# Weights of one product added in SBUF in the last two groups of a two-block kernel, some loads and steps reordered

## The reference

```python
def second_block(x, p, ...):
    h = rmsnorm_2(x, attn_norm_g); proj = h @ w_in
    ...
    merged = sigmoid(g_a) * (y_a @ w_up_a) + sigmoid(g_b) * (y_b @ w_up_b)
    x = x + merged @ w_o
    h = rmsnorm_2(x, ffn_norm_g); hid = h @ w_ffn_in        # 2048 -> 2 * 5632
    x = x + (silu(hid[..., :FFN_HIDDEN]) * hid[..., FFN_HIDDEN:]) @ w_ffn_out
    return x + sigmoid(rmsnorm_2(x, ple_norm_g) @ w_ple_gate) * (p @ w_ple)
```

## Time and profile before

| | |
|---|---|
| median of 3 runs | 1894.41 us (1892.97 to 1895.27) |
| profiled execution, its own time | 1893.05 us |
| its span, first to last instruction | 1891.3 us |
| PE / DVE / ACT / POOL busy | 99% / 78% / 60% / 7% |
| DMA moved | 535.95 MB, mean 283 GB/s |

### The profile page before, as it was taken

How to read it: one execution, slowest core, us unless ns; L and a number is a source line. 1 busy time by engine, 2 the same in 40 slices (tenths; PEclk the granted TensorE clock), 3 DMA queues, 4 the chain that set the end, 5 groups by cost and what they waited for, 6 DMA issues and landing times.

```text
span 1891.3 us, 23371 instructions
## 1 busy us (share of the span) xinstructions
PE 1877.2 (99%) x9018; PEld 1641.9 (87%) x9018; DVE 1471.8 (78%) x1591; ACT 1140.8 (60%) x1417; POOL 130.4 (7%) x156
## 2 busy tenths in 40 slices
PE   9999999999999999999999999999999999999998
PEld 8888888888888888888888888888888888888887
DVE  6889776655666677778888657988998999898865
ACT  7556445555566556566766455666766676666553
POOL 4000011000001100000000000000000000000000
PEclk9999999999999999999999999999999999999999
DMA  9799898999989879998797886788878887987653
GB/s 392 267 284 310 274 309 272 330 347 327 309 290 312 271 269 299 321 315 278 295 313 247 330 256 239 254 311 284 276 254 320 280 271 257 327 260 249 219 188 130
DMA packets 86815, 535.95 MB, mean 283 GB/s; under 512 B 10416, under 2 KB 11184, under 8 KB 40752
## 3 DMA queue, kind: packets, MB, share of 16 engines
q1 hardware_dynamic: 72736, 458.69, 63.3%
q0 software_dynamic: 13824, 75.50, 20.6%
q10 hardware_dynamic: 144, 0.26, 0.0%
HBM read 529.69 MB, written 105.38 MB: 336 GB/s over the span
## 4 chain that ended last, share of the span: by engine, by line
PE 90%; DVE 5%; DMA 3%; issue 1%; ACT 1%; POOL 0%; SPq 0%; ACTq 0%; DVEq 0%; POOLq 0%
PE acc L1359 44%; PE acc L1364 22%; PE aux L1724 12%; PE aux L1728 6%; DVE wlo L2556 2%; PE aux L1338 2%; DMA ple<-in_w_ffn_in 1%; DVE wlo L1876 1%; PE aux L1431 1%; DVE ple L2551 1%; DMA ple<-in_w_in 1%; DMA raw<-summed 1%; PE aux L1805 0%; ACT whi L928 0%; ACT whi L1177 0%
## 5 line engine op out<-in xcount | busy, mean ns | idle before, releaser
L1876 DVE TENSOR_TENSOR wlo<-raw,whi 128x1024 fp32r<-128x1024 f32 x512 | 623.8, 1226 | 296.4 <-ACT whi L928 288.4
L928 ACT ACTIVATE whi<-raw 128x1024 fp32r<-128x1024 f32 x511 | 534.0, 1054 | 449.8 <-PE acc L1364 414.1
L1359 PE MATMUL acc<-whi,actA_hi 128*128 128x512 f32 x892 | 344.0, 386 | 0.7 <-ACT whi L928 0.7
L1359 PE MATMUL acc<-whi,actA_lo 128*128 128x512 f32 x892 | 339.1, 380 | 0.0
L1359 PE MATMUL acc<-whi,actB_hi 128*128 128x512 f32 x796 | 304.5, 383 | 0.2 <-DVE actB_lo L2673 0.2
L1359 PE MATMUL acc<-whi,actB_lo 128*128 128x512 f32 x796 | 301.7, 379 | 0.0
L1177 ACT ACTIVATE whi<-ple 128x1024 fp32r<-128x1024 f32 x192 | 201.0, 1055 | 139.4 <-PE acc L1364 55.6
L2556 DVE TENSOR_TENSOR wlo<-ple,whi 128x1024 fp32r<-128x1024 f32 x192 | 230.2, 1220 | 31.3 <-ACT whi L1177 28.5
L1364 PE MATMUL acc<-wlo,actA_hi 128*128 128x512 f32 x892 | 229.1, 379 | 0.0
L1364 PE MATMUL acc<-wlo,actB_hi 128*128 128x512 f32 x796 | 204.4, 379 | 0.0
L2556 DVE TENSOR_TENSOR wlo<-raw,whi 128x1024 fp32r<-128x1024 f32 x144 | 174.2, 1220 | 30.6 <-ACT whi L1177 28.9
(11 more groups left out here) (366 smaller groups left out, 2377.0 us busy)
## 6 DMA issues: line engine op xcount, KB each, us to landing
raw<-in_w_in SPq DMA_DIRECT2D x108, 1024.0 KB, 7.3
raw<-in_w_ffn_out SPq DMA_DIRECT2D x44, 1024.0 KB, 6.9
summed<-in_w_ffn_in POOLq DMA_DIRECT2D x36, 1024.0 KB, 11.6
raw<-in_w_ffn_in SPq DMA_DIRECT2D x72, 512.0 KB, 7.9
ple<-summed SPq DMA_DIRECT2D x24, 1024.0 KB, 4.9
raw<-summed SPq DMA_DIRECT2D x48, 512.0 KB, 5.4
ple<-in_w_ffn_in SPq DMA_DIRECT2D x18, 1024.0 KB, 6.9
ple<-in_w_ffn_in POOLq DMA_DIRECT2D x36, 512.0 KB, 9.9
```

The source lines that it names most:

```text
L928: act.activation(whi[:, g % RING], raw_piece(g), ACT.Copy).then_inc(hi_ready, 1)
L1359: pe.matmul(acc2(n)[:, t, :], act[x][:, k + c, t * P:(t + 1) * P], woven(whi, g, c), start=(p == 0 and c == 0 and x == 0), stop=False)
L1876: dve.tensor_tensor(wlo[:, g % RING], raw_piece(g), whi[:, g % RING].bitcast(F32), ALU.subtract)\
```

## The change

- For groups 10 and 11, M5's weights are made in `r1` itself: four adding DMAs of b12 per group on POOL's queue, each behind M1's `wlo` of its piece. Their four DRAM sums and four loads are gone; waits count accordingly.
- No DRAM sum is due at the merge's first pieces; the last four sums stay where they were, and POOL no longer looks for due sums in the middle of the groups.
- In the other groups M5's loads are freed by M2's pieces, which puts them behind M7's loads of the same pieces in the SP queue.
- Group 0's M1 load moves up three pieces in the SP list.
- Three orders: the two batches of matmuls that spread the mLSTM rows stand behind two successive pieces, not one; the HGRN2 normalisation of each half moves one piece later on DVE; the product that closes the merge's third slice (`uB`, 2) moves from 3 to 5 pieces behind its slab.

```diff
+ADDED_IN_SBUF = (10, 11)
+SUM_LIST = [(c, n) for c in range(len(BLOCKS)) for n in range(2 if c in ADDED_IN_SBUF else 4)]
+in_sbuf_before = lambda c: len([x for x in ADDED_IN_SBUF if x < c])
...
-                free = {0: self.g_plan + 9, M_GROUPS: self.g_block}.get(c)
+                free = {0: self.g_plan + 6, M_GROUPS: self.g_block}.get(c)
...
-                self.loads.append((self.s_at[c, "M1", 2 * h + 1], self.s_at[c, "M5", 2 * h], "fifth", h, c))
+                if c not in ADDED_IN_SBUF:
+                    self.loads.append((self.s_at[c, "M2", 2 * h + 1], self.s_at[c, "M5", 2 * h], "fifth", h, c))
...
-        SUM_AT += [PLAN.g_plan + 1 + 4 * i for i in range(4)]
-        SUM_AT += [PLAN.g_out + 11 + 6 * i for i in range(4 * S_GROUPS - len(SUM_AT))]
+        SUM_AT += [PLAN.g_out + 11 + 6 * i for i in range(len(SUM_LIST) - len(SUM_AT))]
...
+        M5_DMA = ("b12", "M1")
...
-            eng.wait_ge(sem(f"r1_added{q}"), 16 * (c + 1))
+            eng.wait_ge(sem(f"r1_added{q}"), 16 * (c + in_sbuf_before(c) + 1 + (m == "M4" and c in ADDED_IN_SBUF)))
...
-                        add_in_dram(len([g for g in SUM_AT if g < S_AT[c, "M6", 0]]))
-                        for m, (what, before) in S_DMA.items():
+                        for what, before in ([M5_DMA] if c in ADDED_IN_SBUF else []) + [S_DMA["M4"]]:
                             for q in range(4):
                                 pool.wait_ge(lo_ready, S_AT[c, before, q] + 1)
                                 pool.dma_start(r1[:, q], s_weights(c, what, q), accum_op=ALU.add).then_inc(sem(f"r1_added{q}"), 16)
...
                     if (s, p) == (10, 7):
                         ml_cols()
+                        ml_rows_spread(0)
+                    if (s, p) == (11, 0):
+                        ml_rows_spread(1)
...
-                        if w == L0 + 30:
+                        if w == L0 + 31:
                             powered(dve, f"hB{half}")
...
-                        if g == slab_end(role, j) + (2 if slab_end(role, j) in PLAN.block_end else 3):
+                        last = slab_end(role, j)
+                        if g == last + (2 if last in PLAN.block_end else 5 if (role, j) == ("uB", 2) else 3):
                             u_product(role, j)
```

More of the change, by code:

```diff
@@ L462, in two_blocks_kernel @@
         held_p = nc.dram_tensor("held_p", (P, 2, PK * S), F32, kind="Internal").ap()
-        summed = nc.dram_tensor("summed", (4 * S_GROUPS, P, 4 * COLS), F32, kind="Internal").ap()
+        summed = nc.dram_tensor("summed", (len(SUM_LIST), P, 4 * COLS), F32, kind="Internal").ap()
         SUM_AT = [int(24 + SUM_STEP * i) for i in range(int(116 // SUM_STEP) + 1)] + [144 + 8 * i for i in range(7)]
         SUM_AT += [199 + int(5.4 * i) for i in (0, 1, 2, 3, 8, 9, 10, 11, 12, 13)]
-        SUM_AT += [PLAN.g_plan + 1 + 4 * i for i in range(4)]
-        SUM_AT += [PLAN.g_out + 11 + 6 * i for i in range(4 * S_GROUPS - len(SUM_AT))]
+        SUM_AT += [PLAN.g_out + 11 + 6 * i for i in range(len(SUM_LIST) - len(SUM_AT))]
         acc = ctx.enter_context(nc.psum_tensor("acc", [P, 4, COLS], F32))
@@ L540, in r1_added @@
         def r1_added(eng, c, m, q):
-            eng.wait_ge(sem(f"r1_added{q}"), 16 * (c + 1))
+            eng.wait_ge(sem(f"r1_added{q}"), 16 * (c + in_sbuf_before(c) + 1 + (m == "M4" and c in ADDED_IN_SBUF)))
         def s_weights(c, what, q):
             if what == "seventh":
-                return summed[4 * c + q // 2].rearrange("p (k c) -> p k c", c=COLS)[:, q % 2 * PK:q % 2 * PK + PK, :]
+                return summed[SUM_LIST.index((c, q // 2))].rearrange("p (k c) -> p k c", c=COLS)[:, q % 2 * PK:q % 2 * PK + PK, :]
             k = (KD // 2 if what in ("b22", "b21") else 0) + q * PK
@@ L552, in sum_terms @@
         def sum_terms(i):
-            c, n = divmod(i, 4)
+            c, n = SUM_LIST[i]
             h = 4 * (n % 2)
@@ L778, in load_fifth @@
                 sp.wait_ge(lo_ready, free + 1)
-                summed_in_dram(sp, 4 * c + 2 + h)
-                sp.dma_start(r1[:, 2 * h:2 * h + 2].rearrange("p q k c -> p (q k c)"), summed[4 * c + 2 + h])\
+                i = SUM_LIST.index((c, 2 + h))
+                summed_in_dram(sp, i)
+                sp.dma_start(r1[:, 2 * h:2 * h + 2].rearrange("p q k c -> p (q k c)"), summed[i])\
                     .then_inc(sem(f"r1_loaded{h}"), 16)
@@ L786, in load_half @@
                 if what == "seventh":
-                    summed_in_dram(sp, 4 * c + q // 2)
+                    summed_in_dram(sp, SUM_LIST.index((c, q // 2)))
                 sp.dma_start(raw[:, slot], s_weights(c, what, q)).then_inc(sem(f"half_loaded{slot}"), 16)
@@ L1166, in s_hi @@
             def s_hi(g, c, m, q):
-                if m in ("M1", "M5"):
-                    act.wait_ge(sem(f"r1_loaded{q // 2}"), 32 * c + (16 if m == "M1" else 32))
-                elif m in S_DMA:
+                if m == "M1" or m == "M5" and c not in ADDED_IN_SBUF:
+                    act.wait_ge(sem(f"r1_loaded{q // 2}"), 16 * (2 * c - in_sbuf_before(c) + (1 if m == "M1" else 2)))
+                elif m in ("M5", "M4"):
                     r1_added(act, c, m, q)
@@ L1492, in ml_cols, with ml_rows_spread @@
                 ins.then_inc(aux_full, 1)
[L1493 to L1498, removed]
+            def ml_rows_spread(i):
+                u = AUX[("bc", i)]
+                free(u)
+                for h in range(2):
+                    ins = pe.matmul(bank(u)[:, h * S:(h + 1) * S], sel[:, 2 * i + h, :], hrow[:, 3, :], start=True, stop=True)
+                ins.then_inc(aux_full, 1)
             def ml_scores():
```

## The result

The changed kernel takes 1915.55 us (median of 4, 1911.48 to 1917.74) against 1894.16 before: ratio 1.0111, 95% interval 1.0090 to 1.0131. It is slower by some 21 us, outside the forecast's range. Measured again later beside others, it took 1909.29 (median of 5, 1906.15 to 1911.82), ratio 1.0077 (1.0064 to 1.0090). Lines of the code stand some 6 to 11 further down than before: 1724 is now 1734, 1728 is 1738, 1177 is 1183, 2551 is 2561.

A forecast was written before the change was run, and what follows sets the result against it. PE, busy 99% of the span, bounds the kernel; only its losses between matmuls can be won. Terms summed to −4.4 us, giving 1888.65 from 1893.05 or 1890.0 from the median 1894.41; forecast 1889.4, range 1886.0 to 1894.5.

The forecast's parts named there:

- M5's loads behind M7's in groups 0 to 9: SP's load queue: M7's halves come sooner, b22's first half about half a us later; +0.3 us in all.
- the 1589.7: Predicted landing time in us of b22's first half in group 9, half a us later, leaving a margin of 1.4.
- slow rival: M5's full 5.5 us come ahead of b22's loads, DVE's sum starts late, +16 over nine groups: 1905; chance 0.07.
- (a): HGRN2 normalisation one piece later on DVE: PE's 0.75 us idle at 161.46 goes; −0.8 us.
- (b): mLSTM rows in two batches: the clock fall behind them, from 276 us, goes; −1.6 us.
- (c): `uB` 2 product two pieces later: PE's gap at 1028.58 for `wlo` goes; −0.9 us.
- M7 of group 0: Merge's first group, from 864.46 us: loads no longer delayed by DRAM adds and M5's loads; −1.6 us.
- M4 of group 0: Last quarter, PE idle at 901.18 us: its adding DMA is issued about 0.9 earlier against PE; −1.3 us.
- M1's load three pieces earlier: Group 0 on SP: the load behind it lands about 2.5 us later, still 2 us before its user; 0.
- M5 by adds in group 10: Four adds beside M7's loads: halves take 9.1 us at the first, about 7.5 at the fourth; +1.5 us.
- the rival of all four adds: Group 10: M7's halves wait for all four adds, 9.1 us each to the end, +3.5 or more: 1892; chance 0.18.
- The rival of even turns: Group 10: queues share evenly, M7's loads in time beside the adds, the +1.5 comes back: 1887.9; chance 0.17.

The follow-up runs named there:

- the best version: Changed kernel with M5's loads early, SBUF adds in group 11 alone, group 0's M1 load at its old place, extra sums at pieces 148 and 172: 1889.53 us.

## Why the prediction was wrong, step by step

- **The step that failed: M5's loads behind M7's in groups 0 to 9, put at +0.3; it cost 13 to 24.** Three things in it were wrong. "M7's halves come sooner": only the first does. M5's first load is freed by M2's second piece and so stands between M7's second and third half. "M5's loads overlapped with the halves before as well, so most of the 5.5 was already in those 7.9": that was true in the main of the second load alone. Before, in groups 0 to 9, the first was issued 5 to 7 us ahead of M7's first half and, but for group 0, had landed by then or landed within 1 us; the second was issued 2.3 to 2.6 us ahead. So most of the transfer was new traffic: with both loads behind M7 b22 landed 4.7 us later, not half a us. And the 1589.7 does not come out of its terms. M7's first half of group 9 was issued here:

```profile
1572.75 6.26 SPq L788 DMA_DIRECT2D raw<-summed  x4
```

From there, eight halves and 3 MB at 5.5 us for 2 MB are 19.2 us, so about 1592, 2.7 us later than before; its own slow rival decides from 1.9. The earlier trace rows showed the halves without what stood ahead of them; SP's timeline of one whole group, as above for group 5, tells it.
- **The slow rival** named a real mechanism, but not the one that made the changed kernel slow. With M7 in time and both loads ahead of b22 it cost 11.6 us (b22 +4.7, near its 5.5). In the changed kernel M7, which it lacked, came first, and its sign, DVE's sums with idle time for DMA, did not show in the first record; that its 1905 is near the measured times is luck. Its chance of 0.07 leaned on "M5's loads were in the queue at the same time already", which held for the second of them only.
- **(a)** −0.8: 1.0 gained, 0.3 given back two pieces later, so −0.7. Right.
- **(b)** −1.6: −1.4 at its place, in every record. Right. The other fall, behind 217, cost 1.65 in the changed kernel's record, and it was absent in the one record of the earlier trace rows; the prediction named that weakness.
- **(c)** −0.9: −1.06 in two records with M5's loads early, −0.5 in the best version's and −0.7 with the orders alone. In the changed kernel the 0.6 gained there was lost one piece before, to the late add.
- **M7 of group 0**, −1.6: all of it came with M5's loads early and no sums there, and also with the sums there and M5's loads late (the kernel before with that part alone: 1.0 in its first record, all in its second): either one out of the way was enough. In the changed kernel the first quarter is on time, and M5's load takes 1.1 back at the third:

```profile
863.54 0.38 PE L1734 MATMUL aux<-whi,merge_form_hi 128*128 128x512 f32 x1
...
867.25 0.48 PE L1734 MATMUL aux<-whi,merge_form_hi 128*128 128x512 f32 x1 [0.96 <-ACT whi L1183]
```

- **M4 of group 0**, −1.3: −0.9 to −1.1 with the loads early, as its bounds had it; nothing in the changed kernel's first record, whose stall at M7 had moved to the third quarter. That can't be all: with one or both of M5's loads behind M7's halves M7 was in time, and M4 gained nothing either. The lines are of the changed kernel:

```profile
901.25 0.48 PE L1734 MATMUL aux<-whi,actB_hi 128*128 128x512 f32 x1 [0.96 <-ACT whi L1183]
```

- **M1's load three pieces earlier**, 0: wrong in size. With it the pair behind took 10.6 to 12.3 us, and PE lost some 1.5 in four records that have it and nothing in two, the changed kernel's first among them, nor in any of the seven with the load at its old place. "Still 2 us before its user" was too near.
- **M5 by adds in group 10**, +1.5: 2.5 and 1.2 at M7 in the changed kernel's two records, 0.9 to 1.7 in the three records with M5's loads early or out of M7's way, inside the bounds. M4's 0.2 to 1.0 had not been counted, and 0.6 of it came without adds in group 10 as well. The 9.1 of the earlier trace rows was the right row, and it held to the fourth half, as the rival of all four adds had it: the halves took 8.8 to 9.9. The rival of even turns fell as a price: beside four adds the halves took twice the 4.7 us that they took without. But even turns would have slowed them too, so the "near 0" did not follow. By the earlier trace rows a packet took 0.26 us on q1 and 0.45 on q0 (share times span times 16, by packets); turns of one packet each would leave the loads some 37% of the engines' time while both queues have work, an estimate. The Trainium skill ("DMA: Bandwidth & Descriptors", Queues, rings and completion order) says that a DMA engine takes turns, packet by packet, between the queues that it has work for. No run here shows how the turns went.
- **The sum.** Without the failed step it was −4.7, so 1889.1 from the two bases. The kernel that differs from the changed one in that step alone took 1891.34, 2.2 more; M1's load, put at 0, is some 1.5 of that in its record. The version that beats both took 1889.53, but it also leaves out M1's move and group 10's adds; without their +1.5 the sum would be 1887.6, so that it is near 1889.1 is luck.

## What to carry to other kernels

"Later in the queue" is not "behind": before a load is moved in a queue that is sorted by the piece that frees it, write out the new order of issue of one whole period with times, and look at what used to fill that stretch. A load that finishes early costs nothing where it stands; moved next to loads with a deadline it costs nearly its full transfer time, here 2.3 us per MB where the queue's mean was 2.6, from the point at which their margin ends. And a loss of 0.6 to 5 us, repeated in nine groups, outweighs five careful gains of 1 us.

## What the runs showed of the hardware

- M7's second half took longer where M5's 1 MB was issued 0.42 us behind it on the same queue: 5.8 to 7.2 us on the mean of groups 1 to 9 in the five records with that order, 5.4 to 5.7 in the eight others. The single values scatter: in group 5 it took 7.4 in the changed kernel and 5.3 in the kernel before with that part alone, and 5.2 with M5's loads behind all four halves.
- Four adding DMAs of 512 KB beside four plain loads of 512 KB landed 3.2 to 3.8 us apart, and the first load landed behind three of them. The four loads took 9.6 us at the median against 4.7 without adds.
- The gap of PE of 1.88 us in group 5 was followed by the 1.2 GHz level (0.52 over 1344.5 to 1347), which cost another 1.2. A gap of 1.33 us in group 1 was not: the granted clock stayed at 1.00 from 933.5 to 938.
